# adaLN loads two dense loads ahead on PE, and evacuations ahead of the weight splits on ACT and DVE, in a hybrid diffusion step

## What is computed

```python
mod = silu(cvec) @ w_ada + b_ada            # 2048 x 12288: shift1, scale1, gate1, shift2, scale2, gate2
h = rmsnorm(x, norm1_g) * (1 + scale1) + shift1
p = h @ w_in + b_in                         # 2048 x 8192: u_f | q | k | v | gate_A | gate_B
a = Re(fft2(u_f per group)) @ w_fourier     # 1024 x 2048
b = attention(q, k, v, cached keys, bias) @ w_na_o      # 8 heads of 128; 1024 x 2048
x = x + gate1 * ((sigmoid(gate_A) * a + sigmoid(gate_B) * b) @ w_out)   # 2048 x 2048
h2 = rmsnorm(x, norm2_g) * (1 + scale2) + shift2
x = x + gate2 * moe(h2)                     # 16 experts of 512, two per token, in 4 groups
y = rmsnorm(x, final_norm_g)
```

## Time and profile before

| | us |
|---|---|
| median of 3 runs | 1401.9 |
| lowest, highest | 1396.39, 1405.03 |
| profiled execution | 1407.18 |
| its span | 1405.4 |
| PE busy | 1211.9 (86%) |
| DVE busy | 426.9 (30%) |
| ACT busy | 353.6 (25%) |
| read from HBM | 423.40 MB, 304 GB/s over the span |

### The profile page before, as it was taken

How to read it: one execution, slowest core, us unless ns; L and a number is a source line. 1 busy time by engine, 2 the same in 40 slices (tenths; PEclk the granted TensorE clock), 3 DMA queues, 4 the chain that set the end, 5 groups by cost and what they waited for, 6 DMA issues and landing times.

```text
span 1405.4 us, 14035 instructions
## 1 busy us (share of the span) xinstructions
PE 1211.9 (86%) x5675; PEld 732.0 (52%) x5675; DVE 426.9 (30%) x604; ACT 353.6 (25%) x501; POOL 37.9 (3%) x65
## 2 busy tenths in 40 slices
PE   4787798799889899899999997899888989988782
PEld 2454465566665566676787767543333423333231
DVE  0222254423433244444555544101020211102026
ACT  2322223223223233233344326211001101101012
POOL 0200000000000000000001000000000000000000
PEclk9889898999999999999999997899999999999995
DMA  9998895767554588879866542499999999999994
GB/s 365 313 310 305 295 321 191 254 236 247 207 203 170 216 303 320 290 273 340 308 207 236 181 159 108 162 422 422 421 421 421 421 421 422 421 421 421 421 422 190
DMA packets 111712, 428.26 MB, mean 305 GB/s; under 512 B 8456, under 2 KB 8600, under 8 KB 77216
## 3 DMA queue, kind: packets, MB, share of 16 engines
q1 hardware_dynamic: 107552, 415.26, 77.0%
q0 software_dynamic: 3648, 12.04, 2.9%
q10 hardware_dynamic: 448, 0.07, 0.0%
HBM read 423.40 MB, written 3.93 MB: 304 GB/s over the span
## 4 chain that ended last, share of the span: by engine, by line
PE 53%; DMA 24%; DVE 5%; ACT 2%; issue 1%; SPq 1%; DVEq 0%; ACTq 0%
DMA mraw<-in_w_exp_up 10%; PE bank L628 10%; PE bank L923 10%; PE bank L629 9%; PE bank L630 9%; DMA raw<-in_w_in 6%; DMA mraw<-in_w_exp_down 5%; PE bank L610 4%; PE bank L953 3%; PE bank L877 2%; DMA mraw<-in_w_exp_gate 2%; DVE w_lo L1334 1%; PE bank L765 1%; PE bank L973 1%; ACT w_hi L1062 1%
## 5 line engine op out<-in xcount | busy, mean ns | idle before, releaser
L1334 DVE TENSOR_TENSOR w_lo<-raw,w_hi 128x1024 fp32r<-128x1024 f32 x192 | 232.2, 1223 | 423.8 <-ACT w_hi L1062 422.7
L1062 ACT ACTIVATE w_hi<-raw 128x1024 fp32r<-128x1024 f32 x192 | 199.0, 1055 | 480.9 <-DMA raw<-in_w_in 317.2
L923 PE MATMUL bank<-mraw,xg 128*64 128x512 f32 x1024 | 235.7, 605 | 25.8 <-DMA mraw<-in_w_exp_gate 13.1
L628 PE MATMUL bank<-w_hi,h_hi 128*128 128x512 f32 x512 | 223.7, 437 | 29.7 <-DVE w_lo L1334 29.7
L629 PE MATMUL bank<-w_lo,h_hi 128*128 128x512 f32 x512 | 211.5, 413 | 0.0
L630 PE MATMUL bank<-w_hi,h_lo 128*128 128x512 f32 x512 | 210.3, 411 | 0.0
L923 PEld LDWEIGHTS bank<-mraw,xg 128*64 128x64 f32 x1024 | 76.4, 139 | 163.0 <-issue 161.7
L628 PEld LDWEIGHTS bank<-w_hi,h_hi 128*128 128x128 f32 x512 | 104.0, 203 | 102.6 <-issue 60.0
L953 PE MATMUL bank<-mraw,hidT 128*64 128x512 f32 x512 | 116.4, 597 | 28.9 <-DMA mraw<-in_w_exp_down 28.9
L630 PEld LDWEIGHTS bank<-w_hi,h_lo 128*128 128x128 f32 x512 | 103.2, 202 | 24.2
L629 PEld LDWEIGHTS bank<-w_lo,h_hi 128*128 128x128 f32 x512 | 104.0, 203 | 20.3 <-issue 0.5
(11 more groups left out here) (229 smaller groups left out, 1016.7 us busy)
## 6 DMA issues: line engine op xcount, KB each, us to landing
mraw<-in_w_exp_gate SPq DMA_DIRECT2D x68, 1024.0 KB, 13.5
mraw<-in_w_exp_up SPq DMA_DIRECT2D x68, 1024.0 KB, 13.6
raw<-in_w_in SPq DMA_DIRECT2D x64, 1024.0 KB, 7.3
raw<-in_w_ada SPq DMA_DIRECT2D x64, 1024.0 KB, 4.9
mraw<-in_w_exp_down SPq DMA_DIRECT2D x64, 1024.0 KB, 13.6
raw<-in_w_ada SPq DMA_DIRECT2D x64, 512.0 KB, 8.0
raw<-in_w_out SPq DMA_DIRECT2D x16, 1024.0 KB, 5.1
raw<-in_w_na_o SPq DMA_DIRECT2D x8, 1024.0 KB, 7.2
```

What stands on the lines that cost most here:

```text
L628: nc.tensor.matmul(o, hi[:, k, s], wh, start=k == 0, stop=False)
L923: last = nc.tensor.matmul(out[x * CAP:(x + 1) * CAP], xg[:, q * LOAD_K + kk, e * CAP:(e + 1) * CAP], mraw[:, slot, kk * COL:(kk + 1) * COL ...
L1062: nc.scalar.activation(w_hi[:, u % AHEAD], r, ACT.Copy).then_inc(hi_ready, 1)
L1334: v.tensor_tensor(w_lo[:, u % AHEAD], r, w_hi[:, u % AHEAD].bitcast(F32), ALU.subtract).then_inc(raw_done[n % RAW], 4)
```

## The change

No load, matmul, split or evacuation is added or taken away, and the order of SP's and POOL's queues is the same. What moves:

- In the main loop PE multiplies the adaLN load of two dense loads later (`ADA_LEAD = 2`), between the units instead of ahead of both. In the first group stage two adaLN loads move ahead by one dense load, and `mod_block` stands between the halves of a group's last load. `super_end` and the steps that hang on it come two loads earlier, `mod_super` and `evac_modT` one.
- At the start four of the eight transposes of x come behind `mod_block(0)`, and ACT modulates the first quarter before it copies the rest.
- On ACT and DVE both splits of a turn stand behind what takes PE's results out. `read_chunk`, `normalise` and the odd DFT steps move to the start of the next turn. On ACT `evac_probs` comes a load later.
- On PE `transpose_probs` stands behind the second half of its load. Two waits for `scores_ready` are new.

```diff
@@ -307,9 +307,11 @@
...
+        ADA_LEAD = 2
...
-            return L_MAIN + 16 * (super_chunk - GATE1) + 15 + A_SUPER - A_MAIN
+            return L_MAIN + 16 * (super_chunk - GATE1) + 15 + A_SUPER - A_MAIN - ADA_LEAD
@@ -670,35 +672,48 @@
...
             nc.tensor.transpose(bank[6][:, 0:6 * KD], vecrows[:], ident[0:6 * KD, 0:6 * KD]).then_inc(vecT_done, 1)
-            for b in range(8):
-                if b < 7:
-                    ada_block(0, b + 1)
-                if b == 0:
+            for j in range(1, 8):
+                ada_block(0, j)
+                if j == 1:
                     pe.wait_ge(diag_ready, 1)
+                if j <= 4:
+                    norm_transpose(x0, j - 1, bank[j - 1])
+            mod_block(0)
+            for b in range(4, 8):
                 if b >= 6:
-                    pe.wait_ge(xT_ready, b - 5)
-                norm_transpose(x0, b, bank[b % 6])
-            mod_block(0)
+                    pe.wait_ge(xT_ready, b - 1)
+                norm_transpose(x0, b, bank[b - 2 * (b // 6)])
+            def first_unit(b, ch, half):
+                if half == 0:
+                    if ch == 0:
+                        pe.wait_ge(h_ready, 2 * b + 2)
+                    if b == 0:
+                        pe.wait_ge(xT_ready, (2, 4, 8)[ch])
+                unit(P0_CHUNKS * b + ch, half)
+            ada_block(1, 0)
+            ada_block(1, 1)
             for b in range(4):
...
                     if b < 3:
-                        ada_block(b + 1, 2 * ch)
-                        ada_block(b + 1, 2 * ch + 1)
+                        ada_block(b + 1, 2 * ch + 2)
+                        ada_block(b + 1, 2 * ch + 3)
                     else:
-                        if ch == 0:
-                            ada_super(A_SUPER)
-                        ada_super(A_SUPER + 1 + ch)
-                    if ch == 0:
-                        pe.wait_ge(h_ready, 2 * b + 2)
-                        if b == 0:
-                            pe.wait_ge(xT_ready, 8)
-                    for half in range(2):
-                        unit(P0_CHUNKS * b + ch, half)
-                if b < 3:
-                    ada_block(b + 1, 6)
-                    ada_block(b + 1, 7)
-                    mod_block(b + 1)
+                        ada_super(A_SUPER + 2 + ch)
+                        if ch == P0_CHUNKS - 1:
+                            ada_super(A_SUPER + 3 + ch)
+                    first_unit(b, ch, 0)
+                    if b < 3 and ch == P0_CHUNKS - 1:
+                        mod_block(b + 1)
+                    first_unit(b, ch, 1)
+                if b < 2:
+                    ada_block(b + 2, 0)
+                    ada_block(b + 2, 1)
+                if b == 2:
+                    ada_super(A_SUPER)
+                    ada_super(A_SUPER + 1)
@@ -712,6 +727,8 @@
...
                     nc.tensor.transpose(bank[4][:, m * P:(m + 1) * P], uqkv[:, m // 2, at:at + HD], ident)
+                if h:
+                    pe.wait_ge(scores_ready, h)
                 nc.tensor.transpose(bank[6][:, 0:P], cst[:, j, 0], ident).then_inc(qk_done, 1)
@@ -744,6 +761,7 @@
...
                     pe.wait_ge(chunk_read, 8)
+                    pe.wait_ge(scores_ready, HEADS)
                 if b >= 2:
@@ -791,8 +809,6 @@
...
             for l in range(L_MAIN, L_ALL):
-                if l < L_LAST_ADA:
-                    ada_super(A_MAIN + l - L_MAIN)
                 banks_free(l)
@@ -801,9 +817,9 @@
...
                 unit(l, 0)
+                if l + ADA_LEAD < L_LAST_ADA:
+                    ada_super(A_MAIN + l + ADA_LEAD - L_MAIN)
                 for h in range(HEADS):
-                    if l == HEAD_AT[h] + 2:
-                        transpose_probs(h)
                     if l == HEAD_AT[h] + 3:
@@ -820,13 +836,16 @@
...
                 unit(l, 1)
+                for h in range(HEADS):
+                    if l == HEAD_AT[h] + 2:
+                        transpose_probs(h)
                 if DFT_AT <= l < DFT_AT + 4:
...
                     dft_channels(2 * (l - DFT_AT - 4) + 1)
-                if l == super_end(SHIFT2) + 1:
+                if l == super_end(SHIFT2) + 2:
                     mod_super(0)
-                if l == super_end(SCALE2) + 1:
+                if l == super_end(SCALE2) + 2:
                     mod_super(1)
@@ -1099,13 +1118,15 @@
...
-            for b in range(8):
+            def transposed(b):
...
                 act.wait_ge(norm_done, b + 1)
-                nc.scalar.activation(xT[:, 4 * g:4 * g + 4, s], bank[b % 6][:].rearrange("p (k t) -> p k t", k=4), ACT.Copy
-                                     ).then_inc(xT_ready, 1)
-            act.wait_ge(xT_ready, 8)
+                nc.scalar.activation(xT[:, 4 * g:4 * g + 4, s], bank[b - 2 * (b // 6)][:].rearrange("p (k t) -> p k t", k=4),
+                                     ACT.Copy).then_inc(xT_ready, 1)
+            for b in range(4):
+                transposed(b)
             for b in range(4):
@@ -1113,10 +1134,14 @@
...
                 act.wait_ge(mod_ready, b + 1)
+                act.wait_ge(xT_ready, 4 if b == 0 else 8)
                 for s in range(NS):
...
                     modulate(2 * b + s, lambda k, s, j: xT[:, k, s], 1, 0, 1, s)
+                if b == 0:
+                    for n in range(4, 8):
+                        transposed(n)
                 for u in range(2 * P0_CHUNKS):
@@ -1197,22 +1222,19 @@
...
             for l in range(L_MAIN, L_ALL):
-                if 2 * l + AHEAD < 2 * L_ALL:
-                    high(2 * l + AHEAD)
                 for h in range(HEADS):
-                    if l == HEAD_AT[h] + 2:
+                    if l == HEAD_AT[h] + 3:
                         evac_probs(h)
-                    if l == HEAD_AT[h] + 3:
                         output_high(h)
...
                         evac_qk(h)
+                if DFT_AT + 4 < l <= DFT_AT + 6:
+                    dft_high(2 * (l - DFT_AT - 5) + 1)
                 if DFT_AT <= l < DFT_AT + 4:
...
                     dft_high(2 * (l - DFT_AT - 4))
-                if L_MERGE < l < L_OUT and (l - L_MERGE) % 12 in (4, 8):
-                    sigmoid((l - L_MERGE) // 12 * 2 + (l - L_MERGE) % 12 // 8)
                 if l > L_MERGE + 12 and l <= L_OUT + 1 and (l - L_MERGE) % 12 == 1:
@@ -1223,15 +1245,16 @@
...
                     evac_gate_rows(GATE2, 1)
-                if 2 * l + 1 + AHEAD < 2 * L_ALL:
+                if l >= L_OUT and l % 4 == 3:
+                    gate_rows((l - L_OUT) // 4)
+                if 2 * l + AHEAD < 2 * L_ALL:
+                    high(2 * l + AHEAD)
                     high(2 * l + 1 + AHEAD)
...
                         exponentials(h)
-                if DFT_AT + 4 <= l < DFT_AT + 6:
-                    dft_high(2 * (l - DFT_AT - 4) + 1)
-                if l >= L_OUT and l % 4 == 3:
-                    gate_rows((l - L_OUT) // 4)
+                if L_MERGE < l < L_OUT and (l - L_MERGE) % 12 in (4, 8):
+                    sigmoid((l - L_MERGE) // 12 * 2 + (l - L_MERGE) % 12 // 8)
             act.wait_ge(x1_ready, 4)
@@ -1447,7 +1470,7 @@
...
                 low(2 * L_MAIN + n)
-                if n < P0_CHUNKS:
+                if n < P0_CHUNKS - 1:
                     read_chunk(n)
@@ -1509,11 +1532,18 @@
...
-            for l in range(L_MAIN, L_ALL):
-                if 2 * l + AHEAD < 2 * L_ALL:
-                    low(2 * l + AHEAD)
+            for l in range(L_MAIN, L_ALL + 1):
                 if l == L_MAIN:
+                    read_chunk(P0_CHUNKS - 1)
                     add_mask()
+                else:
+                    chunk, quad, quads = chunk_of(l - 1)
+                    if quad == quads - 1:
+                        read_chunk(chunk)
+                for h in range(HEADS):
+                    if l == HEAD_AT[h] + 2:
+                        normalise(h)
                 for h in range(HEADS):
@@ -1522,28 +1552,23 @@
...
                         attention_low(h)
+                if DFT_AT < l <= DFT_AT + 4:
+                    dft_positions(2 * (l - DFT_AT) - 1)
+                if DFT_AT + 4 < l <= DFT_AT + 6:
+                    dft_low(2 * (l - DFT_AT - 5) + 1)
                 if DFT_AT + 4 <= l < DFT_AT + 6:
...
                     merged_low((l - L_MERGE) // 12 - 1)
-                if l == super_end(SHIFT2) + 2:
+                if l == super_end(SHIFT2) + 3:
                     evac_modT(0)
-                if l == super_end(SCALE2) + 2:
+                if l == super_end(SCALE2) + 3:
                     evac_modT(1)
...
                     finish_mods(2, 3, 5)
-                if 2 * l + 1 + AHEAD < 2 * L_ALL:
+                if 2 * l + AHEAD < 2 * L_ALL:
+                    low(2 * l + AHEAD)
                     low(2 * l + 1 + AHEAD)
-                for h in range(HEADS):
-                    if l == HEAD_AT[h] + 1:
-                        normalise(h)
```

(7 more changed lines are left out.)

## The result

| | before, us | changed, us |
|---|---|---|
| median of the timed runs | 1400.51 (4) | 1329.97 (4) |
| lowest, highest | 1396.39, 1405.03 | 1322.50, 1332.09 |
| profiled execution | 1407.18 | 1322.50 |
| its span | 1405.4 | 1320.7 |

The ratio is 0.9485, interval 0.9444 to 0.9527: 70.5 us less by the medians. A second profile of the changed kernel, taken later, has a span of 1324.2 (1326.01 us, in a set with median 1327.70); where the two differ, both are given.

The account below looks back on a forecast made before the run. Bound: expert transfers, starting when the first part ends; before them, PE waits, low clock and idle queues. Terms 14 + 57 + 6 = 77 us off 1407.2 gave 1330 (1325 from the median); range 1308 to 1354.

Parts of the forecast that it names:

- The part set by the experts' transfers: Expert weights at 421 GB/s: unchanged in length, passing the first part's gain to the end one for one.
- The middle stage: Loads 12 to 41, heads and DFT: 39.0 us of waits and 24 of clock to regain; 57 taken, bounds 40 and 63.
- The 40 us for heads and DFT: Middle stage cross-check: matmuls of heads and DFT would be 40 us beside 200.1 for the loads, leaving 240.
- It costs nothing, its cover is 3 us: Reordered ACT and DVE: splits end about 10 us in, PE wants them at 13 or later; booked at nothing.
- The first stage: First nine loads plus loads 9 to 11: less idle queue between groups, 14 us, bounds 0 and 19.
- the term for loads 9 to 11: End of the first stage: three loads take 22.2 us where 20.0 is clean, so 2 us of gain.
- The 358 GB/s for a core: HBM limit from the Trainium skill, weighed against the first-stage term: by it 9 us; the trace's 388 and 421 GB/s disagreed.
- The rest: Loads 42 to 58: one 3.6 us wait and 3.4 us of clock, 6 taken, bounds 3 and 7; later work 0.
- 1: Heads: cached keys and values land late, seven waits of 3 us plus clock, 32 us less gain, total 1357; chance 0.15.
- 2: First nine loads lose: PE stands before two landings per dense load, term -5 in place of 14, total 1344; chance 0.15.
- 3: Splits on ACT and DVE come too late behind PE's middle-of-load results, 3.5 us a load, total 1430; chance 0.04.
- 4: Change doesn't do what it says: dense loads still land late, waits stay under other names, 1395 to 1405; chance 0.05.

Follow-up runs that it names:

- lead_only: The kernel before with only the main loop's adaLN loads moved two dense loads ahead, between the halves; 1334.91 us, ratio 0.9555.
- evac_only: The kernel before with the changed ACT and DVE order and transpose_probs move, adaLN loads and first stage as before; 1338.69 us, ratio 0.9562.
- prT_mid: The changed kernel with transpose_probs between the halves of its load again and evac_probs one load earlier; 1326.79 us, ratio 0.9457.
- groups_old: The changed kernel with the start and the groups of adaLN blocks put back as before; 1342.88 us, ratio 0.9589.
- pool_late: The changed kernel with POOL's offset-bias loads moved behind the last split of h and add_mask to load 14; 1322.24 us, ratio 0.9432.
- best: The changed kernel with the second group's first two adaLN loads multiplied earlier, POOL's loads out of the first group and add_mask later; 1325.65 us, ratio 0.9462.
- a10_early: The changed kernel with the second group's first two adaLN loads multiplied right behind mod_block(0); 1325.03 us, ratio 0.9445, one execution left out of the ratio.
- pe_only: The kernel before with PE's changed adaLN order (lead of two, new first stage), main-loop ACT and DVE and transpose_probs as before; 1324.89 us, ratio 0.9460.

## Why the prediction held

**The part set by the experts' transfers.** Right: what the ring gained went to the end one for one. 81.7 us by its last matmul (840.2 to 758.5), 84.7 at the end of the span. The 3 us behind the ring are not of the change, see below.

**The middle stage, 57 forecast, 61.0 and 61.3 in the profiles.** The mechanism was right: landings stood in front of steps that did not need them. All 39 us of waits went, 2.5 came new, and the clock is 1.00 where 24 us were booked for it: 242 us where 240 were worked out. I had held back 6 us of 63 for low clock and small waits that did not stay. (The 40 us for heads and DFT are only what 240 leaves beside 200.1, and check nothing.) What the prediction did not say is that the change does this twice over: it reads as if lead, evacuations and the move of the transposes each had a share. `lead_only` and `evac_only` show two ways of which either is enough. The move of the transposes is part of the second; with the lead in place it is not needed (`prT_mid`).

**"It costs nothing, its cover is 3 us".** Right, and the slack is larger: in the head above both splits have ended 11 us after the start of the load in whose turn they stand, and PE wants the first of them after 17 (a load takes longer in a head's turn, 7 to 9 us instead of 6.67). PE never waits for `w_lo` in the middle stage of the changed kernel.

**The first stage, 14 forecast, 12.7 and 10.7.** Inside its bounds of 0 and 19, but made of other pieces. Load 0 started 3.5 us later (3 forecast). The prediction let the first group swallow this and had load 3 at most 1 us later; it came 2.3 and 4.0 us later. PE now takes two adaLN loads more ahead of it, and waits 11.0 us for adaLN landings in this group (1.5 before). The group moved 333 GB/s, where the prediction asked for 350 or more of each. From load 3 to load 12 the forecast was 83.7 us (98.9 less 13.2 for the idle queue and 2 for the last group), and the profiles have 83.9 and 84.2. How it falls on the groups was wrong: the second and third took 31.4 and 26.5 us where 31.6 and 31.9 were forecast, and the term for loads 9 to 11 has the wrong sign, 2 us of gain forecast, 3.8 lost (1.8 in the second profile). In those loads PE stands before two adaLN landings, 4.3 us. The waits of the whole first stage:

```profile
PE bank L596 <- DMA raw<-in_w_ada: 14.9, 10, 3.1
PE bank L612 <- DMA raw<-in_w_ada: 5.0, 3, 2.9
```

Those before L612 are the price of the lead at the border, since the two loads that lead have to be fetched somewhere; the step that was missed is that the last group has to hold one adaLN load more.

The gain itself is less certain than 12.7 and 10.7 sound. Three other kernels have the first stage of before and start load 12 at 184.3 (`lead_only`), 185.5 (`evac_only`) and 183.8 (`groups_old`), 3 to 5 us earlier than the profile of before with its 188.5. Measured from these the new first stage is worth 6 to 10 us up to load 12.

That the first group was bound by POOL's small rows is shown by `pool_late`, and by `best` beside `a10_early`. The 358 GB/s for a core of the Trainium skill (DMA: Bandwidth & Descriptors, "Where 436 GB/s comes from"), weighed there, does not hold here: three windows of the changed kernel have 370 to 372 GB/s over 26 to 31 us.

**The rest, 6 forecast, 6.5 and 1.5.** Loads 42 to 59, for which the 6 stood, gave 6.5. Loads 59 and on, booked at nothing, gave 1.5: the adaLN matmuls of the last two turns (1.06 us a load) are already done there. `evac_only`, which has no lead, takes 226.3 us for these loads, as before.

**The sum.** 77 forecast, 70.5 by the medians of the first set and 73.2 by those of the second (1400.94 to 1327.70), 81 to 85 between profiles. The stages of the ring gave 81.7 and 80.0 us, each within 4.5 us of its forecast. The medians show less because the profiled execution of before lies 6.7 us above its median; 3 to 5 us of that may be the late start of its load 12, the rest was not traced. The prediction took its terms from this one execution. That its 1330 (1407.2 less 77) meets the measured 1329.97 is therefore luck: a saving 6.5 us too large was taken from a time 6.7 us too high.

**The rivals.** 1: its landing did grow, at a twelfth of its price. 2: PE does stand before adaLN landings in the first stage, 19.9 us in 13 waits, and load 3 came later, but loads 3 to 12 gained 15 us at 370 to 372 GB/s. 3 and 4 did not occur; `evac_only` shows that ACT may wait 116 us for dense loads without PE losing more than 4.3.

**What stays open.** The executions of one kernel differ by 3 to 16 us (1325 to 1328 for `prT_mid`, 1333 to 1349 for `lead_only`), and only one of each kernel is profiled, two of the changed one. Differences of a few us between stages of two profiles can be such differences. Part of it is the clock behind the ring, part the first stage; the rest was not traced. The new order on ACT and DVE without the move of the transposes and without the lead was not run.

## What to carry to other kernels

In an engine that works in order, ask of each wait for a transfer what stands behind it: here 176 us of such waits cost the middle stage about 60 because results stood behind them that PE needed soon, and 116 us of them cost almost nothing once PE needed the results later. Two edits that remove one cause from its two ends don't add, so try the smaller one alone first. A lead also has a price where it begins: look there for loads that must now land earlier. And where a stage moves close to its full rate, reordering compute buys only the idle of the queues. The small rows of another queue cost its first group 12 us, but moving them elsewhere gave much of that back, and no gain in the total is shown.

## What the runs showed that I had not expected

Behind the ring every kernel does the same work, yet takes 562.2 to 563.0 us in seven of the fourteen profiles and 564.0 to 566.5 in the other seven, whatever the change. It goes with the clock granted in the second norm and routing, from 20 to 65 us behind the ring: 0.85 in each of the first seven, 0.73 to 0.81 in the others. Before, the changed kernel, its second profile, and `lead_only`:

```profile
860.40:905.40 45.00, 38.23 (x236) 31.99 (x237) 14.71 (x60) 19.64 (x39) 0.53 (x1) 0.77 0.16 53
```

```profile
778.70:823.70 45.00, 37.95 (x247) 30.40 (x248) 14.90 (x61) 19.78 (x40) 0.53 (x1) 0.85 0.18 63
```

```profile
780.40:825.40 45.00, 38.13 (x235) 31.84 (x236) 14.74 (x60) 19.67 (x39) 0.53 (x1) 0.77 0.15 54
```

```profile
791.60:836.60 45.00, 38.00 (x248) 30.45 (x249) 14.90 (x61) 19.78 (x40) 0.53 (x1) 0.85 0.18 62
```

At 0.77 the part takes 565.2 and 564.0, at 0.85 it takes 562.2 and 562.2 (`pe_only`, 0.85, has 562.3; `groups_old`, 0.73, has 566.5). Among the lower ones the clock does not order the times: `best` has 0.81 and 565.2. PE has a gap of 10 us there in every profile, and at which of the two clock levels the pieces between them fall differs from one execution to the next. This is seen in the profiles, and no run changed the clock by itself, so that it is the cause is not shown.
